# Halves of 256 tokens in the last tile of the output projections, the residual and its operand, and in the final scaling and adding

## The chip, the cores and the metric

The kernel runs on one core of one Trainium2 chip. The metric is the device time of one execution in microseconds (us). Lower is better. All times below are in us unless ns is written.

## The reference

Two blocks on a sequence of 512 tokens with 2048 features, batch 1, in float32. What is computed around the change, in short:

```
h = x
y = concat(y_att, y_hg) @ w_out          # 2048 x 2048
h = h + rmsnorm(y, g_post)               # first new residual
gate = sigmoid(h @ w_pg)
e = p @ w_pp
h = h + rmsnorm(gate * e, g_ple)         # second new residual
for l in 0, 1:                           # two layers of the second block
    z = rms_norm(h, pre_norm_g) @ w_in   # 58 tiles of 128 features
    y = mixed(z) @ w_out                 # retention, differential attention, LRU
    h = h + rms_norm(y, post_norm_g)     # third new residual, and after l = 1 the output
```

An rms norm needs the sum of the squares of all 2048 features of a token before the first of them can be scaled.

## The kernel before, in words

Features lie on the 128 partitions, tokens (512) on the free axis. Activations are 16 row tiles `W[:, H + m, :]`; the output of a projection is gathered in `MIX[:, m, :]`, 16 tiles of 128 x 512. Each projection is cut into tiles of 128 output features. A tile is 16 k-steps of three matmuls (high x high, high x low, low x high), as float32 is computed from two float32r parts: `WH`, `WL` for the weights, `UH`, `UL` for the operand. So a tile is 48 matmuls with 512 columns, in four quarters of four k-steps. The tile numbers are T_OUT = 74 to 89 (output of the first block), T_PG = 90 to 105 (gate), T_L2 = 106 onward (68 per layer, the last 16 the layer's output), 242 in all.

The order of work is written out by hand, one program for each engine, with semaphores between them. Every engine works its program in order.

- SyncE (`load`, L229) loads the raw weights of a tile into one of two buffers `RAW`, as soon as the tile two before it has been split (`l_ready`).
- ScalarE converts the high part of a quarter (`high`, L710, which waits for the load and for TensorE to have freed this quarter of `WH`, `w_free`; `high_apart`, L717, writes to separate buffers and waits for the load alone).
- GpSimd subtracts it from the raw weights to get the low part (L262, L270) and signals `l_ready`.
- TensorE's `quarter` (L325) waits for `l_ready`.

At the end of each of the four output stages `out_slots` on ScalarE squares every tile from PSUM (L947) and copies it, times the gain, to `MIX` (L722). VectorE adds the squares to one row `ACC` (`sum_squares`, L1633). The last tile isn't added there: `sum_rows_last` on TensorE multiplies `ACC` (L382) and the last square `SQ1` (L384) by ones, which sums over partitions. `inv_root` on ScalarE (Ln L729, Exp L731) makes the reciprocal root, `ROOT`, in PSUM bank `TP[1]`. In the gate stage ScalarE's `pg_evict` (Exp, L1112) and VectorE's `pg_tile` (add 1, reciprocal L1266, product with e, L1829) come before the square (`pg_square`, L1116).

VectorE's `new_operand` then goes through the 16 tiles, four single ones and six pairs. It multiplies by the root (`scale_tiles`, L1653), drains, adds to the residual (`add_tiles`, L1658, `h_new`). When ScalarE's `operand` has made the high part of the new operand (L916, L918), it subtracts for the low part (`low_tile`, L1616, with gain L1618, `u_ready`). TensorE's `three_tiles` (L341) works on three weight tiles at once, k-step by k-step, as the parts arrive: nine matmuls per k-step, 144 in all. The high parts of the first two of the three tiles are made with `high_apart` ahead of the last output tile's eviction. Those of the third are made by `high`: a first quarter before the root, the others inside `operand`. Also inside `operand` are the quarters of the next tile, as TensorE frees them.

After the second and third new residual ScalarE issues four stores of h (L1154) and squares its 16 tiles (L1158) for the next norm, whose scale is applied to the projections afterwards. VectorE adds them up, and TensorE sums over partitions (L377) in the middle of the fifth tile of the layer. Three spare banks let it go on till then without an eviction.

At the very end VectorE scales tiles 0 to 9 (`scale_tile`, L1647), which GpSimd adds to the residual (`add_residual`, L282) and ScalarE stores (L1243). VectorE scales tiles 10 to 15 into PSUM banks `LAST` (L1915), adds them (L1918), and SyncE stores them (L248).

The few lines by which ScalarE's order is set around the root in the output stages:

```python
if last == "three":
    for x in range(2):
        for q in range(4):
            high_apart(t.plus(16 + x), q, x)
one(t.plus(15), 15, 1, n + 14, quarters=0)
if last == "three":
    high(t.plus(17), 0, t.times(4, 61))
inv_root(OB, row(ACC), D, (sem("sq_used"), PRIMED + n + 16), root, ROOT[:])
```

## Time and profile before

| | us |
|---|---|
| median of 3 runs (lowest to highest) | 3036.14 (3035.97 to 3036.76) |
| the profiled execution | 3036.43 |
| its span, first to last instruction | 3034.6 |
| TensorE matmuls busy in it | 2955.4 (97%), 17162 instructions |
| TensorE weight loads | 2385.6 (79%) |
| VectorE | 1649.8 (54%) |
| ScalarE | 1284.9 (42%) |
| GpSimd | 1315.0 (43%) |
| mean granted TensorE clock | 0.991 |

The share of busy time is an average over the whole span. Matmuls overlap, and the recorded duration of one (0.39 us for 512 columns) is longer than the distance to the next, so distances between starts are used below. In the rows PE is TensorE, PEld its weight loads, DVE VectorE, ACT ScalarE, POOL GpSimd, SP SyncE. A "q" behind the name is the engine's queue, which issues DMAs. L and a number is a line of the kernel. In timeline rows the columns are: start, duration, engine, line, operation, output and inputs, number of merged instructions, and in brackets the idle time of the engine just before and what ended it.

### The profile page before, as it was taken

How to read it: one execution, taken by the hardware profiler on the slowest of the kernel's cores; microseconds unless marked ns; L12 is line 12 of the kernel's file. 1: busy time of each engine (PE TensorE's matmuls, PEld its weight loads, DVE VectorE, ACT ScalarE, POOL GpSimd, SP SyncE). 2: the span in 40 equal slices, each digit the busy share in tenths (PEclk: the TensorE clock that was granted, in tenths of full speed). 3: DMA queues.
4: the chain of work that ended last, by engine and by line, in shares of the span. 5: the costliest groups of instructions: out<-in, count | busy, mean ns of one | idle time of the engine just before them, and what ended most of it. 6: DMA issues, size and time to landing. Idle time of an engine off the chain costs nothing.

```text
span 3034.6 us, 48369 instructions
## 1 busy us (share of the span) xinstructions
PE 2955.4 (97%) x17162; PEld 2385.6 (79%) x17162; DVE 1649.8 (54%) x2349; ACT 1284.9 (42%) x2468; POOL 1315.0 (43%) x1002
## 2 busy tenths in 40 slices
PE   8999999999999999989999999999999999999997
PEld 6888888877777787767887878788778878787886
DVE  5367666655656315657565664561275656654412
ACT  6545444354556333443333333453343333344432
POOL 4444444443433343553444444344444444444444
PEclk9999999999999999999999999999999999999999
DMA  6223222222222323233222222232242222222322
GB/s 238 102 90 111 83 83 76 77 84 83 78 77 80 125 97 139 90 118 125 105 87 91 87 85 82 83 142 100 104 156 88 95 87 96 84 84 80 143 97 97
DMA packets 60880, 305.72 MB, mean 101 GB/s; under 512 B 5712, under 2 KB 6096, under 8 KB 29776
## 3 DMA queue, kind: packets, MB, share of 16 engines
q1 hardware_dynamic: 38224, 259.54, 24.0%
q10 hardware_dynamic: 22528, 44.50, 4.2%
q8 instruction: 77, 1.26, 0.2%
q14 instruction: 51, 0.42, 0.0%
HBM read 285.67 MB, written 18.35 MB: 100 GB/s over the span
## 4 chain that ended last, share of the span: by engine, by line
issue 56%; POOL 32%; PE 9%; POOLq 1%; DMA 1%; ACT 1%; DVE 0%; DVEq 0%; ACTq 0%; SPq 0%
POOL w_low L262 31%; PE z L325 8%; DMA w_raw<-in_wt 1%; POOLq L261 1%; POOL next_weights L270 0%; PE scores L325 0%; PE v_bank L358 0%; PE z L358 0%; ACT u_high L722 0%; DVE mixed L1647 0%; POOLq L296 0%; DVE work L1266 0%; POOLq L284 0%; POOLq L129 0%; ACT w_high L710 0%
## 5 line engine op out<-in xcount | busy, mean ns | idle before, releaser
L262 POOL TENSOR_TENSOR w_low<-w_raw,w_high 128x512 fp32r<-128x512 f32 x932 | 1254.3, 1350 | 1700.0 <-ACT w_high L710 1692.5
L325 PE MATMUL z<-u_high,w_high 128*128 128x512 f32 x3408 | 1347.6, 395 | 2.6 <-POOL w_low L262 1.8
L325 PE MATMUL z<-u_high,w_low 128*128 128x512 f32 x3408 | 1328.4, 390 | 0.0
L325 PE MATMUL z<-u_low,w_high 128*128 128x512 f32 x3408 | 1327.0, 389 | 0.0
L710 ACT ACTIVATE w_high<-w_raw 128x512 fp32r<-128x512 f32 x928 | 578.7, 628 | 1223.0 <-PE z L325 1128.3
L325 PEld LDWEIGHTS z<-u_high,w_high 128*128 128x128 f32 x3408 | 640.1, 188 | 160.2 <-issue 23.3
L325 PEld LDWEIGHTS z<-u_high,w_low 128*128 128x128 f32 x3408 | 639.6, 188 | 136.1
L325 PEld LDWEIGHTS z<-u_low,w_high 128*128 128x128 f32 x3408 | 640.5, 188 | 127.1
L1633 DVE TENSOR_TENSOR work<-work 128x512 f32<-128x512 f32 x87 | 99.9, 1148 | 365.0 <-ACT work L947 351.7
L1260 DVE TENSOR_TENSOR work<-z,work 128x512 f32<-128x512 f32 x110 | 76.1, 692 | 122.7 <-PE z L325 101.8
L1292 DVE SCALAR_TENSOR_TENSOR work<-z,work 32x512 f32<-32x512 f32 (+1 forms) x176 | 120.9, 687 | 2.4
L735 ACT ACTIVATE work<-work 128x512 f32<-128x512 f32 x72 | 45.4, 631 | 145.4 <-DVE work L1272 92.1
L341 PE MATMUL z<-u_high,next_weights 128*128 128x512 f32 x192 | 72.1, 417 | 21.1 <-DVE u_low L1618 13.6
L722 ACT ACTIVATE values_spread<-work 32x512 f32<-32x512 f32 x128 | 80.6, 630 | 19.4 <-DVE work L1449 16.4
L1316 DVE TENSOR_TENSOR work<-o_bank,head_norm 128x512 f32<-128x512 f32 x28 | 19.4, 692 | 112.5 <-ACT head_norm L748 112.5
L1279 DVE TENSOR_TENSOR mixed<-work 128x512 f32<-128x512 f32 (+1 forms) x35 | 24.3, 694 | 85.4 <-ACT work L739 85.4
L1288 DVE SCALAR_TENSOR_TENSOR work<-z,work 128x512 f32<-128x512 f32 x56 | 38.7, 692 | 58.7 <-PE z L325 56.7
L1296 DVE TENSOR_TENSOR work<-work 128x512 f32<-128x512 f32 x56 | 65.4, 1168 | 5.2
L341 PEld LDWEIGHTS z<-u_high,next_weights 128*128 128x128 f32 x192 | 38.5, 200 | 35.5 <-issue 23.4
L1347 DVE TENSOR_TENSOR work<-work 128x512 f32<-128x512 f32 x56 | 55.0, 983 | 18.8 <-ACT work L722 10.8
L722 ACT ACTIVATE work<-work 128x512 f32<-128x512 f32 (+1 forms) x96 | 58.3, 639 | 13.9 <-DVE work L1347 9.7
L1474 DVE SCALAR_TENSOR_TENSOR work<-work 128x512 f32<-128x512 f32 x72 | 60.8, 845 | 6.0 <-issue 0.9
(281 smaller groups left out, 3243.7 us busy)
## 6 DMA issues: line engine op xcount, KB each, us to landing
w_raw<-in_wt SPq DMA_DIRECT2D x241, 1024.0 KB, 4.8
out_hT<-work ACTq DMA_DIRECT2D x8, 1024.0 KB, 8.7
work<-out_hT ACTq DMA_DIRECT2D x8, 1024.0 KB, 10.4
work<-in_xT SPq DMA_DIRECT2D x4, 1024.0 KB, 17.2
e_scratch<-work ACTq DMA_DIRECT2D x1, 4096.0 KB, 16.7
work<-in_xT ACTq DMA_DIRECT2D x4, 1024.0 KB, 10.9
work<-in_dec ACTq DMA_DIRECT2D x12, 256.0 KB, 2.7
work<-rope_tables ACTq DMA_DIRECT2D x10, 256.0 KB, 2.8
```

Of the source, the lines that this page charges most:

```text
L262: pool.tensor_tensor(WL[:, 4 * q:4 * q + 4, :], RAW[:, t.odd, 512 * q:512 * q + 512].rearrange("p (k c) -> p k c", k=4), WH[:, 4 * q:4 * q ...
L325: mm = pe.matmul(bank[:], w[:, k, :], u[:, k, :], start=(k == 0 and n == 0), stop=(k == KT - 1 and n == 2))
L341: mm = pe.matmul(bank[:], w[x], u[:, k, :], start=(k == 0 and n == 0), stop=(k == KT - 1 and n == 2))
L710: act.activation(WH[:, 4 * q:4 * q + 4, :], RAW[:, n.odd, 512 * q:512 * q + 512].rearrange("p (k c) -> p k c", k=4), ACT.Copy).then_inc(se ...
L722: i = act.activation(dst, src, ACT.Copy, **kw)
L735: act.activation(row(r), row(r), ACT.Exp, scale=-1.0)
L1260: v.tensor_tensor(dst, (Z[t.odd] if bank is None else bank)[:], row(RSTD), ALU.mult).then_inc(sem("z_free"), 1)
L1292: i = v.scalar_tensor_tensor(out=row(TM)[o:o + half], in0=z[x:x + half, :], scalar=-scale if first else scale, in1=row(sin)[o:o + half], o ...
L1296: v.tensor_tensor(row(dst), row(dst), row(TM), ALU.add)
L1347: i = v.tensor_tensor(x, x, y, ALU.mult)
L1474: v.scalar_tensor_tensor(out=R_, in0=R_, scalar=-1.0 / f, in1=TB, op0=ALU.add, op1=ALU.mult)
L1633: i = v.tensor_tensor(row(ACC), row(ACC), row(SQ0 + s), ALU.add)
```

## The change

- The last output tile of each output stage and of the gate stage is done by `split_tile`: 48 matmuls for tokens 0 to 255 into one bank, then 48 for tokens 256 to 511 into another. After quarter `at` of the second half comes `sum_first_half`, the sum over partitions of the first half.
- `three_tiles` is done in halves too: first all 16 k-steps with 256 columns, then all again. After k-step `at` of the first half comes `sum_second_half`. Its quarters are freed (`w_free`) in the second half alone.
- ScalarE squares, copies and takes the root half by half (`root_half`). The second half's square and root are interleaved with the first half's operand (`second`).
- VectorE's `new_operand` works in halves: two single tiles and seven pairs, twice.
- At the end all 16 tiles are scaled and added in halves, in pairs: pairs 0 to 4 with GpSimd, 5 to 7 on VectorE. A pair is stored when its second half has been added. Stores are eight of 512 KB instead of four of 512 KB and two of 256 KB from ScalarE, two and two from SyncE.

```diff
-        LAST = [SC[0], SC[1], TP[0], OB, Z[0], Z[1]]
+        LAST = [SC[0], Z[0], Z[1]]
...
+                for half, cols in enumerate(HALVES):
+                    for n in range(pairs):
+                        pool.wait_ge(sem("pair_scaled"), half * pairs + n + 1)
+                        x = W[:, H + 2 * n:H + 2 * n + 2, cols]
+                        i = pool.tensor_tensor(x, x, MIX[:, 2 * n:2 * n + 2, cols], ALU.add)
+                        if half:
+                            i.then_inc(sem("h_new"), 2)
...
+            def three_tiles(t, gen, g, n, at):
+
+                pe.wait_ge(sem("z_free"), t.times(1, -T_HGG - 1))
+                for half, cols in enumerate(HALVES):
+                    for q in range(4):
+                        if half == 0:
+                            pe.wait_ge(sem("l_ready"), t.times(4, 8 + q + 1))
+                        for k in range(4 * q, 4 * q + 4):
+                            if half == 0:
+                                pe.wait_ge(sem("u_half"), g * 16 + k + 1)
+                            else:
+                                pe.wait_ge(sem("u_ready"), gen * 16 + k + 1)
+                            c = slice((k - 4 * q) * P, (k - 4 * q + 1) * P)
+                            hi = [XW[:, r + q, c] for r in XHI] + [WH[:, k, :]]
+                            lo = [XW[:, r + q, c] for r in XLO] + [WL[:, k, :]]
+                            for x, bank in enumerate((Z[0], Z[1], SC[0])):
+                                for i, (w, u) in enumerate(((hi, UH), (hi, UL), (lo, UH))):
+                                    mm = pe.matmul(bank[:, cols], w[x], u[:, k, cols], start=(k == 0 and i == 0),
+                                                   stop=(k == KT - 1 and i == 2))
+                            if half == 0 and k == at:
+                                sum_second_half(n)
+                        if half == 1:
+                            mm.then_inc(sem("w_free"), 3)
+
+            def split_tile(t, n, g, at):
+
+                pe.wait_ge(sem("z_free"), t.times(1, -1 - T_HGG))
+                for half, cols in enumerate(HALVES):
+                    for q in range(4):
+                        if half == 0:
+                            pe.wait_ge(sem("l_ready"), t.times(4, q + 1))
+                        for k in range(4 * q, 4 * q + 4):
+                            for i, (w, u) in enumerate(((WH, UH), (WH, UL), (WL, UH))):
+                                mm = pe.matmul(SPLIT_BANK[half][:, cols], w[:, k, :], u[:, k, cols], start=(k == 0 and i == 0),
+                                               stop=(k == KT - 1 and i == 2))
+                        if half == 1:
+                            mm.then_inc(sem("w_free"), 1)
+                            if q == at:
+                                sum_first_half(n, g)
+                    if half == 0:
+                        mm.then_inc(sem("z_half"), 1)
+
+            def sum_first_half(n, g):
+
+                c = HALVES[0]
+                pe.wait_ge(sem("sq_used"), PRIMED + n + 15)
+                pe.matmul(SUM_BANK[:, c], ONES[:], row(ACC)[:, c], start=True, stop=False)
+                pe.wait_ge(sem("sq_half"), g + 1)
+                pe.matmul(SUM_BANK[:, c], ONES[:], row(SQ1)[:, c], start=False, stop=True).then_inc(sem("sum_half"), 1)
+
+            def sum_second_half(n):
+
+                c = HALVES[1]
+                pe.matmul(OB[:, c], ONES[:], row(ACC)[:, c], start=True, stop=False)
+                pe.wait_ge(sem("sq_ready"), n + 16)
+                pe.matmul(OB[:, c], ONES[:], row(SQ1)[:, c], start=False, stop=True).then_inc(sem("sq_used"), 1)
...
-            sum_rows_last(16)
-            three_tiles(Tile(T_PG), 2)
+            split_tile(Tile(T_OUT + 15), 16, 0, 0)
+            three_tiles(Tile(T_PG), 2, 0, 16, 1)
...
+            split_tile(Tile(T_PG + 15), 32, 1, 2)
...
+                three_tiles(Tile(T_L2 + l * PER_LAYER), l * 2 + 3, l + 1, 64 if l else 32, 1 if l else 4)
...
+                split_tile(Tile(T_L2 + R_OUT + l * PER_LAYER + 15), l * 32 + 64, l + 2, 0)
+            sum_second_half(LAYERS * 32 + 32)
...
+            def root_half(half, wait, done):
+
+                c = HALVES[half]
+                act.wait_ge(*wait)
+                act.activation(row(ACC)[:, c], (OB if half else SUM_BANK)[:, c], ACT.Ln, bias=CS[:, C_EPS:C_EPS + 1], scale=1.0 / D)
+                act.drain()
+                act.activation(ROOTS[half][:, c], row(ACC)[:, c], ACT.Exp, scale=-0.5).then_inc(sem(done), 1)
+
+            def operand(t, g, new, second, scale=None, done=None):
+
+                n = t.times(4)
+                steps = {0: lambda: high(t.plus(1), 1, n - 2), 3: lambda: high(t.plus(1), 2, n - 1), 5: lambda: high(t.plus(1), 3, n)}
+                for half, cols in enumerate(HALVES):
+                    for m in range(KT):
+                        if half:
+                            act.wait_ge(sem("h_new"), m + 1 + new)
+                        else:
+                            act.wait_ge(sem("h_half"), g * 16 + m + 1)
+                        act.activation(UH[:, m, cols], W[:, H + m, cols], ACT.Copy,
+                                       scale=1.0 if scale is None else scale[:, m:m + 1]).then_inc(sem("uh_ready" if half else "uh_half"), 1)
+                        if half == 0 and m in steps:
+                            steps[m]()
+                        if half == 0 and m in second:
+                            second[m]()
+                        if half and m in (7, 11, 13, 15):
+                            q = (7, 11, 13, 15).index(m)
+                            if done is not None:
+                                done(q, *((0, 8), (8, 12), (12, 14), (14, 16))[q])
+                            if q < 3:
+                                high(t.plus(2), q, n + 3 + 3 * q)
...
+                if split is not None:
+                    a = HALVES[0]
+                    act.wait_ge(sem("z_half"), split + 1)
+                    act.wait_ge(sem("sq_used"), PRIMED + n + 14)
+                    act.activation(row(SQ1)[:, a], SPLIT_BANK[0][:, a], ACT.Square).then_inc(sem("sq_half"), 1)
+                    copy(MIX[:, 15, a], SPLIT_BANK[0][:, a], scale=gain[:, 15:16])
+                    if last == "three":
+                        high(t.plus(17), 0, t.times(4, 61))
+                    root_half(0, (sem("sum_half"), split + 1), "root_half")
+
+            def out_second(t, n, gain):
+
+                b = HALVES[1]
+                act.wait_ge(sem("w_free"), t.times(4, 64))
+                act.activation(row(SQ1)[:, b], SPLIT_BANK[1][:, b], ACT.Square).then_inc(sem("sq_ready"), 1)
+                copy(MIX[:, 15, b], SPLIT_BANK[1][:, b], "z_free", scale=gain[:, 15:16])
...
+            act.wait_ge(sem("sq_used"), PRIMED + 32 + 14)
+            pg_evict_half(0, (sem("z_half"), 2), "ze_half")
+            high(Tile(T_L2 + 1), 0, 4 * T_L2 - 3)
+            pg_square_half(0, (sem("pg_half"), 1), "sq_half")
+            root_half(0, (sem("sum_half"), 2), "root_half")
 
             for l in range(LAYERS):
                 three = 4 * (T_L2 + l * PER_LAYER)
-                operand(Tile(T_L2, (PER_LAYER, l)), W[:, H:H + 16, :], PR2[:, l, G2_PRE:G2_PRE + 16], l * 16 + 16,
-                        weights=False, taken=three + 3, third=three if l else None)
+                if l:
+                    second = {2: lambda: out_second(Tile(T_L2 + R_OUT), 64, PR2[:, 0, G2_POST:G2_POST + 16]),
+                              4: lambda: root_half(1, (sem("sq_used"), PRIMED + 80), "root_ready")}
+                else:
+                    second = {1: lambda: pg_evict_half(1, (sem("w_free"), 4 * T_L2), "z_free"),
+                              4: lambda: pg_square_half(1, (sem("pg_prod"), 16), "sq_ready"),
+                              6: lambda: root_half(1, (sem("sq_used"), PRIMED + 48), "root_ready")}
...
+            n = LAYERS * 32 + 32
+            out_second(Tile(T_L2 + R_OUT + (LAYERS - 1) * PER_LAYER), n, PR2[:, LAYERS - 1, G2_POST:G2_POST + 16])
+            root_half(1, (sem("sq_used"), PRIMED + n + 16), "root_ready")
+            for a in range(0, 2 * POOL_PAIRS, 2):
+                act.wait_ge(sem("h_new"), LAYERS * 16 + 16 + a + 2)
+                act.dma_start(out[a:a + 2].rearrange("m p t -> p m t"), W[:, H + a:H + a + 2, :]).then_inc(sem("h_stored"), 16)
+            act.wait_ge(sem("h_stored"), LAYERS * 64 + 16 * POOL_PAIRS)
+            act.wait_ge(sem("last_stored"), 48)
...
+            def new_operand(root, n, g, loaded, scale=None, between={}):
+
+                wait_apart("root_half", g + 1)
                 v.wait_ge(sem("x0_loaded"), 16)
                 v.wait_ge(sem("h_loaded"), loaded)
-                lows = 0
-                for m, k in ((0, 1), (1, 1), (2, 1), (3, 1), (4, 2), (6, 2), (8, 2), (10, 2), (12, 2), (14, 2)):
-                    scale_tiles(m, k)
-                    add_tiles(m, k)
-                    while lows < m:
-                        low_tile(lows, n, W[:, H:H + 16, :], scale)
-                        lows += 1
-                for m in range(lows, 16):
-                    low_tile(m, n, W[:, H:H + 16, :], scale)
+                for half, cols in enumerate(HALVES):
+                    if half:
+                        wait_apart("root_ready", root)
+                    lows = 0
+                    for m, k in ((0, 1), (1, 1), (2, 2), (4, 2), (6, 2), (8, 2), (10, 2), (12, 2), (14, 2)):
+                        b = ROOTS[half][:, cols]
+                        b = bass.AP(b.tensor, b.offset, [b.ap[0], [0, k], [1, S // 2]])
+                        v.tensor_tensor(MIX[:, m:m + k, cols], MIX[:, m:m + k, cols], b, ALU.mult)
+                        v.drain()
+                        x = W[:, H + m:H + m + k, cols]
+                        v.tensor_tensor(x, x, MIX[:, m:m + k, cols], ALU.add).then_inc(sem("h_new" if half else "h_half"), k)
+                        while lows < m:
+                            low_half(lows, n, g, half, scale)
+                            lows += 1
+                        if half == 0 and m in between:
+                            between[m]()
+                    for m in range(lows, KT):
+                        low_half(m, n, g, half, scale)
+
...
+            def pg_last_half(half, wait, done):
+
+                c = HALVES[half]
+                v.wait_ge(*wait)
+                s = row(SQ1)[:, c]
+                v.tensor_scalar(s, s, 1.0, None, ALU.add)
+                v.drain()
+                v.reciprocal(s, s)
+                v.drain()
+                v.tensor_tensor(MIX[:, 15, c], s, MIX[:, 15, c], ALU.mult).then_inc(sem(done), 1)
+
+            pg_last_half(0, (sem("ze_half"), 1), "pg_half")
...
+            for half, cols in enumerate(HALVES):
+                if half:
+                    wait_apart("root_ready", LAYERS + 2)
+                else:
+                    wait_apart("root_half", LAYERS + 2)
+                scaled_pair(0, half)
+                scaled_pair(1, half)
+                for n in range(POOL_PAIRS, KT // 2):
+                    bank = LAST[n - POOL_PAIRS]
+                    scaled_pair(n, half, bank)
+                    v.drain()
+                    x = W[:, H + 2 * n:H + 2 * n + 2, cols]
+                    i = v.tensor_tensor(x, x, bank[:].rearrange("p (m t) -> p m t", m=2), ALU.add)
+                    if half:
+                        i.then_inc(sem("h_last"), 2)
+                    scaled_pair(n - POOL_PAIRS + 2, half)
```

## Rows read from the trace of the kernel before

**Rows 1.** Groups by line, whole span: the first matmuls of each k-step in `three_tiles`.

```profile
L341 PE MATMUL z<-u_high,next_weights 128*128 128x512 f32 x192 | 72.1, 417 | 21.1 <-DVE u_low L1618 13.6 <-DVE u_low L1616 7.5
```

**Rows 2.** Timeline of TensorE, last tile of T_OUT and first of T_PG.

```profile
1160.55 0.39 PE L325 MATMUL z<-u_high,w_low 128*128 128x512 f32 x1
...
1168.43 0.77 PE L341 MATMUL z<-u_high,next_weights 128*128 128x512 f32 x1 [5.68 <-DVE u_low L1616]
...
1206.11 0.39 PE L325 MATMUL scores<-u_high,w_high 128*128 128x512 f32 x1
...
1211.78 0.39 PE L325 MATMUL scores<-u_low,w_high 128*128 128x512 f32 x1
```

**Rows 3.** Timeline of VectorE in the first new residual.

```profile
1164.87 0.69 DVE L1653 TENSOR_TENSOR mixed<-mixed,turned 128x512 f32<-128x512 f32 x1 [12.16 <-ACT turned L731]
...
1194.21 1.21 DVE L1653 TENSOR_TENSOR mixed<-mixed,turned 128x1024 f32<-128x1024 f32 x1
1195.50 1.23 DVE L1658 TENSOR_TENSOR work<-work,mixed 128x1024 f32<-128x1024 f32 x1
...
1199.39 1.96 DVE L1616 TENSOR_TENSOR u_low<-work,u_high 128x512 fp32r<-128x512 f32 x2 [1.47 <-ACT u_high L916]
```

**Rows 4.** Timeline of ScalarE before the first new residual.

```profile
1157.14 2.19 ACT L717 ACTIVATE next_weights<-w_raw 128x512 fp32r<-128x512 f32 x4 [3.21 <-DMA w_raw<-in_wt]
...
1162.90 0.63 ACT L710 ACTIVATE w_high<-w_raw 128x512 fp32r<-128x512 f32 x1 [0.75 <-DMA w_raw<-in_wt]
```

**Rows 5.** Timeline of TensorE's weight loads in a retention head.

```profile
1485.21 0.97 PEld L518 LDWEIGHTS scores<-work 128*128 128x128 f32 x8
```

**Rows 6.** Timeline of all engines at the end of the span.

```profile
3013.72 1.02 PE L382 MATMUL o_bank<-work,ones 128*128 128x512 f32 x2
...
3017.17 2.48 DVE L1647 TENSOR_TENSOR mixed<-mixed,turned 128x512 f32<-128x512 f32 x4 [11.53 <-ACT turned L731]
3018.06 8.67 POOL L282 TENSOR_TENSOR work<-work,mixed  x7 [12.96 <-DVE mixed L1647]
...
3020.58 10.88 ACTq L1243 DMA_DIRECT2D out_hT<-work  x6
```

**Rows 7.** Page, costliest groups, whole span: GpSimd's low parts.

```profile
L262 POOL TENSOR_TENSOR w_low<-w_raw,w_high 128x512 fp32r<-128x512 f32 x932 | 1254.3, 1350 | 1700.0 <-ACT w_high L710 1692.5
```

**Rows 8.** Timelines of ScalarE, VectorE and TensorE around the second new residual.

```profile
1347.28 2.18 ACT L717 ACTIVATE next_weights<-w_raw 128x512 fp32r<-128x512 f32 x4
1350.25 0.60 ACT L1112 ACTIVATE work<-z 128x512 f32<-128x512 f32 x1 [0.80 <-PE z L325]
1352.08 2.19 ACT L710 ACTIVATE w_high<-w_raw 128x512 fp32r<-128x512 f32 x4 [1.23 <-DMA w_raw<-in_wt]
...
1352.09 3.35 DVE L1266 RECIPROCAL work<-work 128x512 f32<-128x512 f32 x1
...
1361.62 0.69 DVE L1653 TENSOR_TENSOR mixed<-mixed,turned 128x512 f32<-128x512 f32 x1 [4.27 <-ACT turned L731]
...
1368.78 0.75 DVE L1618 SCALAR_TENSOR_TENSOR u_low<-work,params,u_high 128x512 fp32r<-128x512 f32 x1
...
1400.94 0.39 PE L325 MATMUL scores<-u_high,w_high 128*128 128x512 f32 x1
```

**Rows 9.** Timeline of TensorE around the third new residual.

```profile
2184.47 1.02 PE L382 MATMUL o_bank<-work,ones 128*128 128x512 f32 x2
...
2230.22 0.39 PE L325 MATMUL scores<-u_high,w_high 128*128 128x512 f32 x1
```

**Rows 10.** Timelines of ScalarE and TensorE behind the second new residual.

```profile
1397.54 1.76 ACT L1158 ACTIVATE work<-work 128x512 f32<-128x512 f32 x3 [2.63 <-issue]
...
1418.22 1.12 PE L377 MATMUL o_bank<-work,ones 128*128 128x512 f32 x2 [0.80 <-DVE work L1633]
```

**Rows 11.** Stretch at the end: engines' busy us, granted clock, DMA share, GB/s.

```profile
3024.00:3026.00 2.00, 0.00 (x0) 0.00 (x0) 1.93 (x5) 0.00 (x0) 2.00 (x3) 0.50 1.00 378
```

**Rows 12.** The same view, the stretch behind the first new residual's idle time.

```profile
1168.40:1173.70 5.30, 5.27 (x13) 4.14 (x14) 5.15 (x7) 1.83 (x4) 1.75 (x1) 0.50 0.00 0
```

151 lines of the change are left out of this document (56 added, 95 removed).

## The prediction

> **What bounds the kernel now.** I read, in this order, the groups by line, the timeline of each engine through the three new residuals and the end, and the stretches with their clock. TensorE works nearly the whole span; what it loses in `three_tiles` (line 341) is 21.1 us of recorded idle time, all of it waiting for the low parts of the operand, which VectorE writes [rows 1]. So each stage is asked: when does VectorE begin, how long does it need, and who is behind it?
>
> I count each stage from T, the start of its last tile. A matmul takes 0.227 us ((1211.78 - 1206.11) / 25 [rows 2]), a tile of 48 takes 10.9. In stage 1 (after T_OUT) the last matmul starts at 1160.55, so T = 1149.9. TensorE gets its first operand at T+18.5 and finishes `three_tiles` at T+56.2 (1206.11) [rows 2], though 144 matmuls need only 32.7. VectorE begins at T+15.0 (1164.87) and ends its last low part at T+51.5 (1199.39 + 1.96) [rows 3]. What gates its start is ScalarE: before the root it converts a quarter of weights, which waits for a load of w_raw until 1162.90 = T+13.0. Its earlier group of four conversions, for the second tile ahead, also waits for a load, from T+4 until 1157.14 = T+7.2 and is through at T+9.4 [rows 4].
>
> **The change, part by part.**
> *Halved matmuls.* 48 become 96 in four tiles, 144 become 288 in three stages. The nearest row is eight loads of 128x128 weights in 0.97 us, one per 0.11 us, each with a 192 ns load in flight [rows 5]; their fp32 128-column matmuls run at the same pace. I take 0.113, half of 0.227: no cost. The bounds are 0.107 and 0.19 (loads that don't overlap).
>
> *The earlier start, stage 1.* The first half is ready at T+5.7. But in ScalarE's order the group of four comes first: T+9.4, where TensorE, which stands at the sum after the first quarter, idles from about T+7.2 to T+9.8. Then the quarter of weights still stands ahead of `root_half`, and its load still comes at T+13.0, as nothing before it is changed. Today VectorE starts 1.97 us after that quarter starts (1162.90 to 1164.87 [rows 3, 4]). Ln and Exp on 256 columns save 0.27 each: VectorE starts at **T+14.4, 0.5 earlier, no more**. The half norm is computed early and waits in the queue.
>
> *VectorE's work.* An operation on 512 columns is 0.69, on 1024 1.21 [rows 3]: 0.52 per 512 and 0.17 fixed. Followed closely it costs 0.08 less (2.48 for four [rows 6]); a drain behind it adds 0.16 (1194.21 to 1195.50 is 1.29 [rows 3]). Today: 4 single tiles x (0.77 + 0.61) + 6 pairs x (1.29 + 1.13) + 16 lows x 0.61 = 29.8. After, for one half: 2 x (0.50 + 0.34) + 7 x (0.77 + 0.61) + 16 x 0.34 = 16.8, for both **33.6: 3.8 more**. Today's stretch is 36.5 = 29.8 + 1.5 of waiting for ScalarE [rows 3] + 5.2, which I put down to GpSimd: six of its low-part operations, of 1.35 in the mean [rows 7], fall into it (the last three quarters of the third tile, the first three of the next), 0.87 each; two lows then take 1.96 instead of 1.3. Six fall into it after the change too. Bounds are 0.5 (most of it under the scaling, which reads PSUM) and 1.35 (all of it).
>
> The Trainium skill (SBUF — State Buffer, "Who interferes with whom") says that a VectorE operation with two SBUF inputs and a GpSimd operation that reads SBUF block each other for the whole instruction. By that rule alone each costs up to 1.35, and the sum below would be 8.6 higher; the trace shows the block, but 0.87.
>
> *Stage 1.* T+14.4 + 33.6 + 5.2 + 0.4 at the end = T+53.6. TensorE then has nine half matmuls: T+54.7 against T+56.2, **-1.5**. TensorE itself, fed at T+16.5, would be through at T+50: VectorE is the bound, with halves more than before. On ScalarE the 32 halved UH copies (0.63 less 0.27, as its 512-column conversions take 0.63 [rows 4]) and the second half's square and root lie beside VectorE's work.
>
> *Stage 2 (after T_PG).* ScalarE's Exp reads the last tile at 1350.25, 0.2 after TensorE leaves it: T = 1339.2. The second group of four conversions starts at 1347.28 and ends at T+10.3; only then comes `pg_evict_half`. The reciprocal of 3.35 [rows 8] becomes 1.7: the product is there at T+14.3, having passed the quarter that waits for its load (1352.08 = T+12.9 [rows 8]); square, sum, root: VectorE starts at T+16.4, against T+22.4 (1361.62). Gain 6 there. But its work is 33.6 + 32 x 0.06 for the scaled lows (0.75 against 0.69 [rows 3, 8]) + 2.7 for the second half's sigmoid in between + 5.2 for GpSimd, of which three operations are new in this stretch, + 1.2 of waiting for the seventh UH tile behind `root_half(1)` + 0.4 = 45.0. TensorE is through at T+62.4, against T+61.8 (1400.94 [rows 8]): **+0.6**.
>
> *Stage 3 (after layer 0).* As stage 1 with scaled lows: T+14.3 + 41.1 + 1.1 = T+56.5; today 2230.22 - (2184.47 - 10.9) = T+56.6 [rows 9]: **-0.1**.
>
> *Behind stages 2 and 3.* Today VectorE is done some 5 us before TensorE, and uses it: the squares start at 1397.54, 3.4 before TensorE ends `three_tiles`, and still the sum matmul (line 377) holds TensorE 0.8 at 1418.22 [rows 10]. With halves VectorE finishes about 1.1 before TensorE. The same four DMA issues on ScalarE's queue then put the squares at 0.7 after it, 4.1 later; some 1.6 of it is won back, since ScalarE no longer waits there for TensorE's quarters. **+2.5 each**, between 0 and 4.1. In order behind line 377 stand two and a half tiles, so it moves the end.
>
> *The end.* T = 3013.72 - 10.9 = 3002.8. No weights stand in the way here. Half 1 is normed at T+8.9; VectorE needs 2 x 0.61 + 3 x 1.98 = 7.2 for each half and is done at T+23.2 instead of T+28. GpSimd adds five pairs per half at 1.24 (8.67 for seven [rows 6]) and is done at T+24.6. But no tile can be stored before its second half: the first issue is at T+18.8; today it is at 3020.58 = T+17.8 [rows 6]. The DMA engines move 378 GB/s when full [rows 11], so 4.19 MB need 11 us. Today they start 0.3 after the first issue, are nearly full, and the span ends 2.0 after them (3034.6). After: 18.8 + 0.3 + 10.9 + 2.0 = T+32.0 against T+31.8: **+0.2**. The transfer bounds the end; the arithmetic's 4 us vanish in it.
>
> **The sum:** -1.5 + 0.6 - 0.1 + 2.5 + 2.5 + 0.2 = +4.2. The profiled execution took 3036.43 (span 3034.6), 0.3 above the median of 3036.14: 3040.6, or 3040.3 as a median.
>
> **Rivals.**
> 1. *Slower: the clock.* In line 377's wait, now 3.5, TensorE's clock falls. After the idle stretch before 1168.43 (5.7 [rows 2]) it ran 5.3 us at a granted clock of 0.50, 1.2 GHz, and 13 matmuls filled them, which take 3.0 at 0.227: 2.3 lost [rows 12]. After 0.8 (1418.22) it did not. If 3.5 is already enough, 2 x 2.3: 3044.9. It decides from a wait somewhere between 0.8 and 5.7. Chance 0.2.
> 2. *Slower: weight loads bound half matmuls.* At 0.19, 288 take 55: TensorE ends at T+72, about +16 in each stage, 3085 or more. The eight loads at 0.11 [rows 5] speak against it. 0.04. GpSimd blocking VectorE for a full 1.35, 18 x 0.48 more, gives 3048.9: 0.1, as it is 0.87 today.
> 3. *Faster: VectorE isn't held up.* Short operations let GpSimd in under the scaling: 0.5 for 18 operations saves 6.6; and the squares catch up, 5.0. +4.2 - 11.6 = 3028.7. For it: 37% of VectorE's time is scaling. Against: a block falls on adds and lows, the rest. 0.14.
> 4. *Nothing:* only one of these two savings: 3034 to 3035.5. 0.15.
> My forecast has the remaining 0.37, its own range 3036 to 3045.
>
> **Numbers.** A measurement of this kernel can tell 0.2%, 6.1 us, from no change. The range 3031 to 3049 leaves out the far ends of rivals 2 and 3. Faster 0.15 is rival 3 and the edge of rival 4. Slower (over 3042.2) gets most of rivals 1 and 2, 0.28, and a quarter of my own: 0.37. The same: 0.48.
>
> **What would show it.** Right: ScalarE's first half Ln in stages 1 and 3 directly behind a quarter that waited for a DMA, at T+13.5; TensorE idle inside the last tile; VectorE's operations at 0.42 and 0.69; line 377 waiting about 3.5 us; DMA full from T+19 to T+30 at the end. Wrong: a root at T+9 in stage 1, or VectorE done 5 us ahead of TensorE, or half matmuls over 0.13.

## The result, and the profile after

The changed kernel takes 3046.77 us (median of 7 runs, 3045.0 to 3050.19), the kernel before 3036.26 beside it (7 runs, 3035.97 to 3037.99). The ratio is 1.0035, with a 95% interval of 1.0025 to 1.0046: slower by 10.5 us (by the interval 7.6 to 14.0), where 4.2 were forecast. The profiled execution took 3045.98, its span is 3044.2 against 3034.6, TensorE's mean granted clock 0.992 against 0.991. In two of the comparisons below a few executions ran at a clock of 0.57 to 0.85 throughout and took some 270 us or more longer; they are left out.

I count again from T, the start of a stage's last tile. First the timeline of TensorE and VectorE through stage 1 of the changed kernel, which answers to [rows 2, 3]. L366 is the halved tile, L381 the end of the first half's sum, L350 `three_tiles`, L329 the next tile:

```profile
1149.42 0.28 PE L366 MATMUL turned<-u_high,w_high 128*128 128x256 f32 x1
...
1155.17 0.28 PE L366 MATMUL v_bank<-u_high,w_high 128*128 128x256 f32 x1
...
1159.09 0.70 PE L381 MATMUL scores<-work,ones 128*128 128x256 f32 x2 [1.88 <-ACT work L1019]
...
1163.61 0.42 DVE L1758 TENSOR_TENSOR mixed<-mixed,turned 128x256 f32<-128x256 f32 x1 [11.39 <-ACT turned L953]
...
1165.84 0.36 PE L350 MATMUL z<-u_high,next_weights 128*128 128x256 f32 x1 [0.25 <-DVE u_low L1780]
...
1200.60 1.65 DVE L1780 TENSOR_TENSOR u_low<-work,u_high 128x256 fp32r<-128x256 f32 x2 [1.18 <-ACT u_high L967]
...
1204.22 0.40 PE L329 MATMUL scores<-u_high,w_high 128*128 128x512 f32 x1
```

T is 1149.42. VectorE starts at T+14.2, TensorE gets its first operand at T+16.4 and is through at T+54.8, against T+56.2 before. A half matmul follows the one before it after 0.120 us (5.75 for 48), not 0.113.

Stage 2, the timelines of TensorE, ScalarE and VectorE, answering to [rows 8, 10]. L755 is ScalarE's conversion of a quarter of weights, L967 that of the operand, L1241 the squares:

```profile
1337.20 0.28 PE L366 MATMUL turned<-u_high,w_high 128*128 128x256 f32 x1
...
1351.85 1.22 PE L381 MATMUL scores<-work,ones 128*128 128x256 f32 x2 [3.98 <-ACT work L1215]
...
1354.13 0.42 DVE L1758 TENSOR_TENSOR mixed<-mixed,turned 128x256 f32<-128x256 f32 x1 [2.78 <-ACT turned L953]
...
1370.23 0.49 DVE L1782 SCALAR_TENSOR_TENSOR u_low<-work,params,u_high 128x256 fp32r<-128x256 f32 x1 [1.99 <-ACT u_high L967]
...
1396.80 0.63 ACT L755 ACTIVATE w_high<-w_raw 128x512 fp32r<-128x512 f32 x1 [3.04 <-PE scores L350]
1397.33 0.90 ACT L967 ACTIVATE u_high<-work,params 128x256 fp32r<-128x256 f32 x2
...
1397.86 1.62 DVE L1782 SCALAR_TENSOR_TENSOR u_low<-work,params,u_high 128x256 fp32r<-128x256 f32 x2 [1.07 <-ACT u_high L967]
...
1400.47 1.76 ACT L1241 ACTIVATE work<-work 128x512 f32<-128x512 f32 x3 [2.25 <-issue]
1401.39 0.40 PE L329 MATMUL scores<-u_high,w_high 128*128 128x512 f32 x1
```

TensorE is through at T+64.2, against T+61.8. ScalarE's last two conversions of the operand stand behind a quarter of weights that waits 3.04 us for TensorE, and the squares start 0.9 before TensorE leaves the stage; before they started 3.4 before it.

Behind stages 2 and 3, the timeline of TensorE, first of the kernel before behind its wait at line 377 (stage 2), then of the changed kernel. L422 is what was line 377:

```profile
1418.79 0.79 PE L325 MATMUL turned<-u_high,w_high 128*128 128x512 f32 x1
...
1420.81 0.39 PE L325 MATMUL turned<-u_low,w_high 128*128 128x512 f32 x1
```

```profile
1421.87 1.47 PE L422 MATMUL o_bank<-work,ones 128*128 128x512 f32 x2 [3.97 <-DVE work L1718]
1422.43 1.33 PE L329 MATMUL turned<-u_high,w_high 128*128 128x512 f32 x1
1423.56 0.63 PE L329 MATMUL turned<-u_low,w_high 128*128 128x512 f32 x1
...
1426.05 0.40 PE L329 MATMUL turned<-u_low,w_high 128*128 128x512 f32 x1
...
2179.22 0.28 PE L366 MATMUL turned<-u_high,w_high 128*128 128x256 f32 x1
...
2235.62 0.40 PE L329 MATMUL scores<-u_high,w_high 128*128 128x512 f32 x1
...
2254.67 1.41 PE L422 MATMUL o_bank<-work,ones 128*128 128x512 f32 x2 [2.54 <-DVE work L1718]
```

And stretches of the changed kernel: length, busy time of each engine, then the granted clock, the DMA share and GB/s. The first lies in the wait behind stage 2, the next two stand behind the waits of stages 2 and 3, and the last is where the first of these two is over:

```profile
1419.00:1421.90 2.90, 0.03 (x1) 0.03 (x1) 2.48 (x3) 1.88 (x4) 1.98 (x2) 1.00 0.57 162
1421.90:1426.10 4.20, 4.20 (x10) 2.84 (x11) 0.00 (x0) 0.22 (x1) 2.28 (x2) 0.59 0.89 296
2255.20:2258.90 3.70, 3.70 (x10) 2.57 (x9) 0.00 (x0) 0.00 (x0) 1.77 (x2) 0.54 0.89 327
1426.10:1430.00 3.90, 3.90 (x19) 3.23 (x18) 0.47 (x1) 1.85 (x3) 1.29 (x1) 1.00 0.08 34
```

The waits are 4.0 and 2.5 us, where each was 0.8, and behind each matmuls start every 0.43 us for about 3 us: the clock's lower level, 1.2 GHz. From 1422.43 to 1426.05, seven steps from one matmul to the next, it takes 3.6 us; the same seven took 2.0 before (1418.79 to 1420.81). So each wait costs another 1.6.

At the end, the queues of ScalarE and SyncE (L1328, L250) and two stretches, answering to [rows 6, 11]:

```profile
3012.06 0.28 PE L366 MATMUL turned<-u_high,w_high 128*128 128x256 f32 x1
...
3031.17 6.30 ACTq L1328 DMA_DIRECT2D out_hT<-work  x5
3031.22 4.24 SPq L250 DMA_DIRECT2D out_hT<-work  x3
```

```profile
3031.00:3032.00 1.00, 0.00 (x0) 0.00 (x0) 1.00 (x3) 0.00 (x0) 1.00 (x2) 0.50 0.00 0
...
3034.00:3036.00 2.00, 0.00 (x0) 0.00 (x0) 1.59 (x3) 0.00 (x0) 1.30 (x2) 0.50 1.03 376
```

T is 3012.06. The first store is issued at T+19.1 and the span ends at T+32.1, against T+31.8.

Put together, the span's 9.6 us are:

| stretch | forecast | measured |
|---|---|---|
| ahead of stage 1 (nothing changed there) | 0 | -0.5 |
| stage 1 | -1.5 | -1.4 |
| stage 2 | +0.6 | +2.4 |
| stage 3 (2235.62 - 2179.22 = 56.4, was 56.6) | -0.1 | -0.2 |
| from a stage's end to line 422, stages 2 and 3 | +5.0 | +3.2, +1.8 |
| half clock behind line 422 | 0 | +1.6, +1.6 |
| the end | +0.2 | +0.4 |
| the two long stretches of the layers between | 0 | +0.8 |

### The profile page after: what moved, and what is told of

Read it like the earlier page. It is cut to its first block, busy times and chain, and to the rows that moved or that the text cites. A ratio compares the mean times of both kernels' runs of the same rounds, so it can differ in the third digit from the quotient of the medians.

```text
span 3044.2 us, 49558 instructions
## 1 busy us (share of the span) xinstructions
PE 2970.9 (98%) x17802; PEld 2428.2 (80%) x17802; DVE 1660.2 (55%) x2448; ACT 1296.7 (43%) x2533; POOL 1316.6 (43%) x1002
## 4 chain that ended last, share of the span: by engine, by line
issue 56%; POOL 32%; PE 9%; POOLq 1%; DMA 1%; ACT 1%; DVE 0%; DVEq 0%; ACTq 0%; SPq 0%
POOL w_low L264 31%; PE z L329 8%; DMA w_raw<-in_wt 1%; POOLq L263 1%; POOL next_weights L272 0%; PE scores L329 0%; PE v_bank L403 0%; PE z L403 0%; ACT u_high L767 0%; PE turned L366 0%; POOLq L300 0%; DVEq L2052 0%; DVE work L2054 0%; DVE work L1351 0%; POOLq L288 0%
## 5 line engine op out<-in xcount | busy, mean ns | idle before, releaser
L329 PE MATMUL z<-u_high,w_high 128*128 128x512 f32 x3344 | 1322.7, 396 | 2.5 <-POOL w_low L264 1.7
L329 PE MATMUL z<-u_high,w_low 128*128 128x512 f32 x3344 | 1303.6, 390 | 0.0
L329 PE MATMUL z<-u_low,w_high 128*128 128x512 f32 x3344 | 1302.2, 389 | 0.0
L755 ACT ACTIVATE w_high<-w_raw 128x512 fp32r<-128x512 f32 x928 | 579.0, 628 | 1222.0 <-PE z L329 1126.8
L329 PEld LDWEIGHTS z<-u_high,w_high 128*128 128x128 f32 x3344 | 628.1, 188 | 157.5 <-issue 23.3
L329 PEld LDWEIGHTS z<-u_high,w_low 128*128 128x128 f32 x3344 | 627.7, 188 | 133.8
L329 PEld LDWEIGHTS z<-u_low,w_high 128*128 128x128 f32 x3344 | 628.4, 188 | 124.6
L350 PE MATMUL z<-u_high,next_weights 128*128 128x256 f32 x384 | 89.6, 295 | 10.0 <-DVE u_low L1782 8.0
L767 ACT ACTIVATE values_spread<-work 32x512 f32<-32x512 f32 x128 | 80.6, 630 | 19.5 <-DVE work L1534 16.5
L350 PEld LDWEIGHTS z<-u_high,next_weights 128*128 128x128 f32 x384 | 67.9, 195 | 14.3 <-DVE u_low L1782 8.9
L1373 DVE SCALAR_TENSOR_TENSOR work<-z,work 128x512 f32<-128x512 f32 x56 | 38.7, 692 | 58.0 <-PE z L329 56.1
L1432 DVE TENSOR_TENSOR work<-work 128x512 f32<-128x512 f32 x56 | 55.0, 983 | 18.8 <-ACT work L767 10.8
```

The source lines that it names most:

```text
L329: mm = pe.matmul(bank[:], w[:, k, :], u[:, k, :], start=(k == 0 and n == 0), stop=(k == KT - 1 and n == 2))
L350: mm = pe.matmul(bank[:, cols], w[x], u[:, k, cols], start=(k == 0 and i == 0), stop=(k == KT - 1 and i == 2))
L755: act.activation(WH[:, 4 * q:4 * q + 4, :], RAW[:, n.odd, 512 * q:512 * q + 512].rearrange("p (k c) -> p k c", k=4), ACT.Copy).then_inc(se ...
L767: i = act.activation(dst, src, ACT.Copy, **kw)
L1432: i = v.tensor_tensor(x, x, y, ALU.mult)
```

## The experiments

Each kernel was run 6 to 11 times beside the kernel before on the same chip. Over the comparisons the kernel before took 3036.0 to 3036.8, so a difference between kernels of two comparisons carries up to 0.8. A trace is of one execution, and a stage's length differs between them even where no edit touches it: stage 1 took 54.7 to 56.1 in the changed kernel, e1, e6b, e7b and e8, stage 2 64.2 to 65.0 in the changed kernel, e1 and e6b, stage 3 56.3 to 57.7 in the same five as stage 1. Edits are against the changed kernel where nothing else is said.

**e1_sum_later.** TensorE's sum behind stages 2 and 3 two quarters later, and ScalarE's root that reads it one quarter later.

```diff
-                        if m == 4 and q == 1:
+                        if m == 4 and q == 3:
                             sum_rows(row(ACC), OB, ...
-                        if m == 4 and q == 2:
+                        if m == 4 and q == 3:
                             inv_root(OB, row(RSTD), ...
```

> The changed kernel, with the sum matmul behind stages 2 and 3 (line 422) set two quarters (24 matmuls, 5.4 us) later in TensorE's order, and the root that reads it on ScalarE moved by one quarter. Theory A (the loss is that wait and the clock behind it): the waits of 4.0 and 2.5 us vanish, and with them the 1.6 us that TensorE's half clock costs behind each: 3046.8 - 6.5 - 3.2 = 3037.1 us, ratio to the kernel before 1.000, no row of 0.42 us a matmul behind line 422. Theory B (VectorE needs the root and is late itself, so that TensorE waits later for the banks of the next tiles instead): waits of some 4 us appear further on and the time stays near 3045, ratio 1.003. Theory C (waits go, but the clock does not depend on them): 3040.3.

Measured 3038.55, ratio 1.0006 (0.9997 to 1.0015), 8.2 below the changed kernel. Its timeline of TensorE behind stage 2, and the stretch that follows:

```profile
1426.05 1.02 PE L422 MATMUL o_bank<-work,ones 128*128 128x512 f32 x2
1426.50 0.80 PE L329 MATMUL turned<-u_high,w_high 128*128 128x512 f32 x1
```

```profile
1426.10:1430.10 4.00, 4.00 (x17) 2.95 (x16) 1.34 (x2) 2.12 (x4) 2.48 (x2) 1.00 0.53 183
```

No wait, and the clock stays at 1.00. From the end of stage 2 to T of stage 3 it takes 772.5 against 777.8, from the end of stage 3 to T of the last tile 771.9 against 776.4: 9.8 together, near theory A's 9.7. A wait of 0.7 for GpSimd stands in the way once. Theory B is out, and so is C, by the clock's row. The whole span is 8.1 shorter (3036.1 against 3044.2), not 9.8: ahead of stage 1 it stands 1.0 behind, and stage 2 takes 65.0 instead of 64.2, two places that the edit doesn't touch.

**e2_before_sum_later.** The same edit on the kernel before.

> The kernel before with the same move of its sum matmul (line 377). It waits 0.8 us there twice and then shows two matmuls at half clock. Theory A: 2 x (0.8 + 0.6) = 2.8 less, 3033.4 us, ratio 0.9991. Theory B: no change, ratio 1.000, with the waits further on.

3034.21, ratio 0.9994 (0.9985 to 1.0003). 1.8 less, in the direction of theory A, where 2.8 were expected. The interval doesn't exclude no change, though the single executions (3033.6 to 3035.0) all lie below those of the kernel before beside them (3035.3 to 3038.1); its trace has no wait at the sum.

**e3_root_first.** ScalarE's first half root ahead of the quarter of weights.

```diff
-                    if last == "three":
-                        high(t.plus(17), 0, t.times(4, 61))
                     root_half(0, (sem("sum_half"), split + 1), "root_half")
+                    if last == "three":
+                        high(t.plus(17), 0, t.times(4, 61))
```

and the same for `high(Tile(T_L2 + 1), 0, ...)` in stage 2.

> The changed kernel with ScalarE's quarter of weights, whose load lands at T+12.7 (T is the start of a stage's last tile), moved behind the first half's root. Theory A (the root only queued behind that load): VectorE starts at T+10.5 to T+11 instead of T+14.2 in stage 1, near that in stage 3 and T+14 instead of T+16.9 in stage 2; as VectorE's work bounds the stages, TensorE ends each 2.5 to 3 us earlier: 3046.8 - 8 = 3039, ratio 1.0008. Theory B (TensorE bounds instead: its last tile ends at T+16.4, the second half's root comes no earlier and its low parts neither): VectorE starts earlier and waits for the second root, each stage gains 0 to 1: 3045 to 3046.8, ratio 1.003. The wait at line 422 stays under both.

3046.47, ratio 1.0034 (1.0021 to 1.0046): theory B. Stage 1, timelines of VectorE and TensorE (T = 1150.14):

```profile
1161.75 0.42 DVE L1758 TENSOR_TENSOR mixed<-mixed,turned 128x256 f32<-128x256 f32 x1 [8.81 <-ACT turned L953]
1162.25 1.19 DVE L1761 TENSOR_TENSOR work<-work,mixed 128x256 f32<-128x256 f32 x1
...
1166.65 0.36 PE L350 MATMUL z<-u_high,next_weights 128*128 128x256 f32 x1 [0.16 <-DVE u_low L1780]
...
1204.65 0.40 PE L329 MATMUL scores<-u_high,w_high 128*128 128x512 f32 x1
```

VectorE starts at T+11.6, 2.6 earlier: what held the root was indeed the load. But an add of 0.43 takes 1.19 there, beside GpSimd's low parts of the last tiles, TensorE still has its last tile until T+16.5, and the stage ends at T+54.5, 0.3 earlier. Stage 2 ends at T+65.4, 1.2 later, stage 3 at T+55.3, 1.1 earlier. None of the three is clear of the spread between executions.

**e4_uh_first.** In the second half's conversions, the third quarter of weights behind tiles 14 and 15.

```diff
-                            if q < 3:
+                            if q in (0, 1):
                                 high(t.plus(2), q, n + 3 + 3 * q)
+                            if q == 3:
+                                high(t.plus(2), 2, n + 9)
```

> The changed kernel with ScalarE's third quarter of weights for the second tile ahead, which waits 3.0 us for TensorE, moved behind the last two conversions of the operand. Theory A (this wait delays the last low parts by 1.1 us and the squares behind stages 2 and 3 by 3): each stage ends about 1 us earlier, the squares start 2.5 us earlier, line 422 waits 4.0 - 1.5 and 2.5 - 1.5: 3046.8 - 3 - 3 - up to 1.6 of the clock = 3040, ratio 1.001. Theory B (the squares wait for TensorE's quarters anyway, as each fourth is followed by a conversion that does): squares start earlier but the sum ends as now: 3044 to 3046, ratio 1.003.

3046.60, ratio 1.0033 (1.0020 to 1.0045): theory B in the total. Stage 2 (T = 1336.79), timelines of VectorE, ScalarE's queue and ScalarE, and TensorE:

```profile
1395.12 1.67 DVE L1784 SCALAR_TENSOR_TENSOR u_low<-work,params,u_high 128x256 fp32r<-128x256 f32 x4
...
1396.45 3.13 ACTq L1239 DMA_DIRECT2D out_hT<-work  x3
1399.63 1.76 ACT L1243 ACTIVATE work<-work 128x512 f32<-128x512 f32 x3 [2.97 <-issue]
...
1400.07 0.40 PE L329 MATMUL scores<-u_high,w_high 128*128 128x512 f32 x1
```

VectorE is done at T+60.0 instead of T+62.3, yet TensorE only at T+63.3 instead of T+64.2: what is left then are TensorE's own matmuls. In stage 1 it is the same: VectorE T+50.6, TensorE T+54.2, 0.6 earlier (54.2 to 54.3 also in e5b, x1 and x2, which have this edit). Stage 3 ends 0.6 later. The squares come only 0.4 earlier, since now the issue of the four stores holds them: the wait at line 422 is 4.5 and 3.0.

**e5b_stores_between.** e4, and the stores between the squares.

```diff
-                for g in range(4):
-                    act.dma_start(out[4 * g:4 * g + 4]...).then_inc(sem("h_stored"), 16)
                 for m in range(KT):
                     act.wait_ge(sem("sq_used"), ...)
                     act.activation(row(SQ0 + m % 2), row(H + m), ACT.Square)...
+                    if m % 4 == 3:
+                        g = m // 4
+                        act.dma_start(out[4 * g:4 * g + 4]...).then_inc(sem("h_stored"), 16)
```

> As e4_uh_first, and the four stores of h on ScalarE's queue behind stages 2 and 3, after which the squares started in e4_uh_first (2.97 us idle for their issue), set one by one behind each fourth square. Theory A (the sum is late because the squares start late): squares start at T+60 in stage 2, 3 us earlier than with the change, the sum's last add ends 2 to 3 us earlier and line 422 waits about 1.5 and 0.5 us instead of 4.0 and 2.5; with waits that short the clock stays up: 3046.8 - 5 - 3.2 = 3038.5, ratio 1.0006. Theory B (an issue costs the same wherever it stands, and the squares are paced by VectorE's adds): squares start earlier, but end as now, 3046, ratio 1.003.

3037.65, ratio 1.0004 (0.9995 to 1.0013): theory A. Timelines of ScalarE and TensorE behind stage 2, and the stretch behind the wait:

```profile
1397.08 1.13 ACT L1240 ACTIVATE work<-work 128x512 f32<-128x512 f32 x2
...
1418.22 1.12 PE L422 MATMUL o_bank<-work,ones 128*128 128x512 f32 x2 [1.14 <-DVE work L1721]
```

```profile
1418.30:1422.30 4.00, 4.00 (x16) 2.97 (x17) 0.00 (x0) 1.25 (x3) 2.55 (x2) 1.00 1.02 323
```

Squares from T+60.2 (T = 1336.92), waits of 1.1 and 0.8, clock 1.00. So two different edits, one that takes the consumer out of the way (e1, 8.2) and one that makes the data earlier (e5b, 9.1 with e4's edit in it, which alone gave 0.2), each bring back 8 to 9 us.

**e7b_s2_sum_late.** `split_tile(Tile(T_PG + 15), 32, 1, 3)`: the first half's sum behind the whole last tile.

> The changed kernel with the first half's sum in stage 2 one quarter (12 matmuls) later, behind the whole last tile. Theory A (the 4.0 us that TensorE waits there cost the clock: the last quarter runs at half speed, so the second half's product, root and low parts come late): TensorE runs 12 matmuls in 1.4 us ahead of the wait, which shrinks to 2.5, and ends three_tiles at T+63.2 or earlier instead of T+64.2: 3045.8, ratio 1.0031. Theory B (the stage is bound by VectorE's work and the first root, which this doesn't change): T+64.2 as now, 3046.8, ratio 1.0035. If the sum itself is late: T+65.

3047.02, ratio 1.0032 (1.0020 to 1.0044). Nothing is gained in time. The wait at L381 shrinks to 2.6 and the sum stands at T+14.7 as before, but in the trace the stage ends at T+65.1, 0.9 later, which neither theory had for a sum that isn't late. The same stretch of stage 2, from T+19.2 for 6.5 us, first in the changed kernel, then in e7b, then in e1, whose stage 2 is that of the changed kernel:

```profile
1356.40:1362.90 6.50, 4.34 (x18) 3.98 (x18) 6.20 (x10) 2.20 (x6) 2.34 (x2) 0.64 0.00 0
```

```profile
1360.00:1366.50 6.50, 4.33 (x18) 3.99 (x18) 6.21 (x10) 2.19 (x6) 2.41 (x2) 0.50 0.00 0
```

```profile
1357.46:1363.96 6.50, 4.34 (x18) 3.98 (x18) 6.20 (x10) 2.19 (x6) 2.34 (x2) 0.50 0.00 0
```

The same work at a lower clock. In e7b TensorE has its last tile behind it, waits 3.35 us between the sum and the operand, and stays at the lower level until T+31.5; the second half's sum comes at T+31.5 instead of T+30.4, and ScalarE's second root waits 4.5 instead of 3.6 for it. So the clock reaches the end of stage 2 through that root, for 0.8 to 0.9 (e6b, with stage 2 unchanged and the clock at 0.66 in this stretch, ends it at T+64.2). But that the moved sum brought the lower clock on isn't shown: e1, with the sum in its old place, has the same 0.50, its second sum at T+31.4 and the same end, T+65.0.

**e6b_end_halves.** Stores of the last output by halves: eight more on SyncE's queue.

```diff
+            c = HALVES[0]
+            for name, count, a in (("end_pool", 1, 0), ("end_last", 1, 10), ...):
+                sp.wait_ge(sem(name), count)
+                sp.dma_start(out[a:a + 2]...[:, :, c], W[:, H + a:H + a + 2, c])...
```

> The changed kernel with the last output stored by halves: each pair of tiles is stored in its first 256 tokens as soon as these are ready (SyncE's queue), its second 256 after the second half. Theory A (the transfer bounds the end, since it starts only at T+19.1 and then takes 11 us): 2.1 MB are out before T+20 and the span ends about 3 us after the last sum on GpSimd (T+25), at T+28 instead of T+32.1: 3046.8 - 4 = 3042.8, ratio 1.0022. Theory B (rows of 1 KB instead of 2 KB move at half the rate, or eight more issues on SyncE's queue hold up the second halves): the end stays at T+32 or later: 3046.8 to 3051, ratio 1.0035 or more.

3042.42, ratio 1.0018 (1.0009 to 1.0027): theory A, 4.4 less. `c` is the first half's columns; the stores behind the second half carry the other half alone. SyncE's queue, GpSimd's last sum, and a stretch:

```profile
3024.10 6.68 SPq L252 DMA_DIRECT2D out_hT<-work  x8
3031.62 4.31 SPq L256 DMA_DIRECT2D out_hT<-work  x3
...
3036.27 1.26 POOL L290 TENSOR_TENSOR work<-work,mixed 128x512 f32<-128x512 f32 x1 [0.70 <-DVE mixed L2046]
```

```profile
3034.00:3036.00 2.00, 0.00 (x0) 0.00 (x0) 1.93 (x4) 0.00 (x0) 1.33 (x2) 0.50 1.04 342
```

The span ends at 3040.2, T+27.7 (T = 3012.52), 2.7 behind the last sum: now the arithmetic bounds the end, and the 4 us that halves save in it count.

**e8_s2_whole.** Stage 2 undone: its last tile, norm, residual and `three_tiles` as before, the other three in halves. **e9_only_end.** The reverse for the end: the three residuals as before, only the last output in halves. Both edits take the functions of the kernel before under another name and call them in those stages.

> The changed kernel with stage 2 (behind T_PG) undone: its last tile, norm, residual and three_tiles whole as before, the other three places in halves. Theory A (stage 2's halves are a net loss in themselves and bring on the long wait behind it): TensorE ends three_tiles at T+61.8 instead of T+64.2, line 422 waits 0.8 there instead of 4.0 and loses 0.4 instead of 2.0 by the clock: 2.4 + 3.2 + 1.6 = 7.2 less, 3039.6 us, ratio 1.0011. Theory B (halves in stage 2 only move work, and what they lose there is caught by other waits): less than 3 us come back, 3044 or more, ratio 1.0025.

> The end's part of the change alone: the last output tile, its norm and the final adding in halves; the three residuals whole as before. Theory A (the transfer bounds the end and starts a little later): the end takes T+32.1 instead of T+31.8, the rest is as before: 3036.6, ratio 1.0001. Theory B (the change's loss sits in the end too): 3038 or more. Theory C (the 4 us of arithmetic do count): 3032.5.

e8: 3038.46, ratio 1.0005 (0.9995 to 1.0014), theory A. TensorE behind stage 2 (T = 1337.15), timeline:

```profile
1398.57 0.39 PE L329 MATMUL scores<-u_high,w_high 128*128 128x512 f32 x1
...
1415.85 1.13 PE L445 MATMUL o_bank<-work,ones 128*128 128x512 f32 x2 [0.80 <-DVE work L1767]
```

T is 10.9 before 1348.03, where the sum behind its whole last tile starts. TensorE is through at T+61.4, and the wait is 0.8 again. Stage 2 alone, with the wait that it brings on, holds 8.3 of the 10.5 us. e9: 3036.26, ratio 1.0000 (0.9991 to 1.0009). Theory C is out; A and B's 3038 both lie inside the interval, and the trace, with its end at T+32.1, is theory A's. The end costs and gives nothing that can be measured.

**Three combinations.** x1_all is e1, e5b (with e4's edit in it), e6b and e7b together; x2_all_s2_whole is e1, e5b and e6b with stage 2 whole; x3_end_and_sum is e1 and e6b with all three residuals whole.

> The changed kernel with all of e1 (sum matmul later), e4 and e5 (conversions and stores out of the way of the squares), e6 (stores by halves at the end) and e7 (stage 2's sum later). If the waits are separate costs, the savings that each run shows add up: e1 gave 8.2, e4 0.2, and e5's share of the wait is already taken by e1; with e6's 4 and e7's 1: 3046.8 - 8.2 - 0.5 - 4 - 1 = 3033, ratio 0.999, faster than both kernels. If the end does not gain: 3037, ratio 1.0003.

> x1_all without its part e7 and with stage 2 whole as in e8_s2_whole. In x1_all TensorE ended stage 2 at T+64.0, against T+61.8 before the change, and its sum matmul waited for nothing already. Theory A: only the 2.2 us of the stage itself come back: 3030.7 - 2.2 = 3028.5, ratio 0.9973. Theory B (no gain, as the operand ends when it does by VectorE's work and the rest is hidden): 3030.7, ratio 0.998.

> The kernel before with two things: the sum matmul behind stages 2 and 3 two quarters later (as e2, which gave 1.8) and the end in halves, stored by halves (as e6, which gave 4.4 against the change's own end, itself 0.4 behind). The residuals are all whole. Theory A (the parts add; in x2_all_s2_whole the halves of stages 1 and 3 were through at T+54.2 and T+55.75 against T+56.2 and T+56.6, so they were worth 2.9 there): 3036.3 - 1.8 - 4.0 = 3030.5, ratio 0.9981, some 3 above x2_all_s2_whole. Theory B (the halves of stages 1 and 3 bring nothing that stays): 3027, as x2_all_s2_whole.

| | us | ratio | 95% |
|---|---|---|---|
| x1_all | 3030.71 | 0.9980 | 0.9971 to 0.9989 |
| x2_all_s2_whole | 3027.05 | 0.9969 | 0.9958 to 0.9980 |
| x3_end_and_sum | 3030.22 | 0.9979 | 0.9970 to 0.9988 |

All three are faster than the kernel before, by 0.2 to 0.3%. x1 is 2.3 below what was expected, and some 3.5 below what e1 and e6b give alone; this wasn't taken apart. Stage 2 whole is worth 3.7 (x1 to x2, 2.2 expected), and halves in stages 1 and 3, with the edits of e4 and e5b, are worth 3.2 (x3 to x2, 2.9 expected). The single executions of x2 (3026.3 to 3028.6) lie below those of x1 and x3 (from 3029.1), but the intervals of the ratios overlap.

## Why the prediction was right, and where it was not

The forecast had the direction of each part, and its range of 3031 to 3049 holds the result. But the sum was 4.2 and the measurement 10.5, and 3046.8 lies above the forecast's own narrower range (3036 to 3045): the wide range held it because it made room for rivals. Step by step:

- **Halved matmuls, "no cost".** The pace is 0.120 us. That is 0.013 for each old matmul, 1.9 for a `three_tiles`, hidden as long as VectorE is the bound. e4 shows the cover running out: with VectorE 2.2 us faster TensorE gains 0.6 to 0.9. "TensorE itself would be through at T+50" was too low: 288 at 0.120 take 34.6, so it is T+52 at the least (an estimate from the start at T+16.4, with some 0.7 for the second half's sum), and in e4, where it still waited 0.66 and 0.71, it was T+54.2.
- **Stage 1.** Start T+14.2 (forecast 14.4), TensorE idle 1.9 in the last tile (2.6), end T+54.8 (54.7): right, but the end's closeness is partly luck. VectorE was through at T+52.8, not T+53.6, as GpSimd held it less, though it waited 1.2 for ScalarE's last two conversions. TensorE then needed 2.0, not 1.1: the last two low parts come about 0.3 apart, a k-step takes it 1.08, and it had two to do, not one. The errors cancel. e3 confirms what the root queued behind, and also that this didn't matter.
- **GpSimd's hold on VectorE.** In stage 1 the six held operations lose 4.1 us in all (adds of 1.05 for 0.69, pairs of lows of 1.86, 1.84 and 1.65 for 0.75), against 5.2 forecast. By the Trainium skill (SBUF — State Buffer, "Who interferes with whom") the shared port pair is an exclusive lock, which for operations of 1.35 on GpSimd makes up to 1.35 a time (an estimate from that rule and rows 7). The rows show the hold, with 0.35 to 1.1 for each.
- **Stage 2, +0.6: mis-sized, +2.4.** VectorE starts 0.5 late (T+16.9), waits 2.0 instead of 1.2 for the seventh conversion (it stands behind a root that waits for a TensorE at 0.64 of its clock), and waits 1.1 for ScalarE's last two, which stand behind a quarter that waits for TensorE: that wait I had not listed. GpSimd holds it 4.2, not 5.2, so it is through 0.9 late, at T+62.3. TensorE ends 1.9 behind the last low part, not 1.0, as in stage 1. With e4's edit the stage ended at T+63.3; without halves in stage 2 (e8) at T+61.4.
- **Stage 3.** -0.2 for -0.1: right, though executions differ by more than that.
- **Line 422, +2.5 each.** 3.2 and 1.8, 5.0 together as forecast, but by luck. The squares were to start 4.1 later against TensorE's end, with 1.6 of it won back. They start 2.5 and 2.4 later (0.9 before that end in both stages, where it was 3.4 and 3.3), and from there to the sum it takes 0.7 more in stage 2 and 0.6 less in stage 3. What holds them, DMA issues ahead of the squares on ScalarE's queue, was right: it is what e5b removed.
- **The clock: the step that failed.** The sum put it at nothing; it was rival 1, at a chance of 0.2, and is worth 3.2 us of the 10.5. The rows left open from which wait on it decides, between 0.8 and 5.7; with waits of 3.5 forecast, that was no case for 0.2. And the trace of the kernel before could have narrowed it. It has a wait of 4.2 us elsewhere, and behind it the clock reads 0.50 (a timeline row of TensorE and the stretch behind it; after another wait, of 3.9 at 999.03, it falls to 0.50 as well):

```profile
962.66 2.08 PE L474 MATMUL scores<-work 64*128 64x512 f32 x4 [4.21 <-DVE work L1302]
```

```profile
962.70:964.00 1.30, 1.30 (x4) 0.47 (x4) 1.12 (x2) 0.02 (x1) 0.00 (x0) 0.50 0.00 0
```

Its price was over the mark: 1.6 for each, not 2.3.

- **The end.** First issue T+19.1 (18.8), end T+32.1 (32.0): right. Two small terms were not, and cancel: the DMA engines start 1.0 after the first issue (0.3 in the sum), and the span ends 1.0 after them (2.0). "The transfer bounds the end" is shown by e6b, and e9 shows the part alone at nothing.

The remaining 0.3 (-0.5 and +0.8 in stretches that the change doesn't touch) isn't explained; executions of one kernel differ by more. That the large terms are causes and not only a sum of one trace rests on e1, e5b and e8.

## What to carry to other kernels

In this kernel, halving a chain of steps helped only the engine that bounds it, and lengthened the work of each engine in it: before halving, see who is next, here TensorE 2 us behind VectorE. When a change makes a packed TensorE wait longer at one instruction, look in the trace that you already have for other waits of that length and read the clock behind them. Then ask whether the instruction can stand a little later: the cheapest edit of the study, a sum moved by 24 matmuls, gave back 8.2 us. Arithmetic made faster ahead of a full transfer gave nothing here until the transfer was cut up in the same way; then it gave 4.4. And before a change of 1 us in a stage's length is put down to an edit, compare executions that the edit doesn't touch there.
